# Attention pairs interleaved on TensorE, group factors taken ahead of the output product, and two moved steps in the second block, in a two-block transformer kernel

## What is computed

```python
h = rms_norm(x, g_mix_norm[l])
z = h @ w_in[l]                      # latents, rope key, u and v of a gating unit, pool input
a  = mla_mixer(...)                  # 4 heads of causal softmax attention, width 512
gm = sgu_mixer(uv, ...)              # u * (W @ rms_norm(v) + b), width 256
po = pool_mixer(pin, ...)            # windowed means, then a 64x64 product per group, width 256
mix = concatenate([rms_norm(a, g1), rms_norm(gm, g2), rms_norm(po, g3)])
x = x + mix @ w_out[l]
h = rms_norm(x, g_ffn_norm[l])
x = x + (silu(h @ w_gate[l]) * (h @ w_up[l])) @ w_down[l]
```

## Time and profile before

| | us |
|---|---|
| median of 3 runs | 3214.23 (3213.72 to 3214.51) |
| the profiled execution | 3211.73 |
| its span in the profile | 3209.9 |
| PE busy | 3129.9 (98%) |
| POOL busy | 1905.3 (59%) |
| DVE busy | 1486.2 (46%) |
| ACT busy | 736.1 (23%) |

### The profile page before, as it was taken

One profiled execution on the slowest core, in us unless ns is written; L12 is line 12 of the kernel. 1 busy time (PEld: TensorE's weight loads), 2 busy tenths in 40 slices (PEclk: granted clock), 3 DMA queues, 4 the chain that ended last, 5 costly groups with the idle time before them and its releaser, 6 DMA issues.

```text
span 3209.9 us, 41968 instructions
## 1 busy us (share of the span) xinstructions
PE 3129.9 (98%) x15408; PEld 2512.8 (78%) x15408; DVE 1486.2 (46%) x2570; ACT 736.1 (23%) x1521; POOL 1905.3 (59%) x885
## 2 busy tenths in 40 slices
PE   8899999989999999999999999999999999999998
PEld 7588888868888878877588888887787658888887
DVE  4654530365543033886554555212288654554521
ACT  4410000432010032434711101012243470111000
POOL 4267777427787777001078777787700118877785
PEclk9999999999999999999999999999999999999999
DMA  3122333113223222112022232232211202333232
GB/s 122 47 94 93 97 98 98 54 46 100 93 97 98 96 83 96 48 40 73 14 90 94 101 98 97 93 99 86 92 47 34 79 10 97 99 101 97 93 98 85
DMA packets 71716, 262.99 MB, mean 82 GB/s; under 512 B 8208, under 2 KB 8208, under 8 KB 71440
## 3 DMA queue, kind: packets, MB, share of 16 engines
q1 hardware_dynamic: 71280, 258.86, 24.8%
q10 hardware_dynamic: 288, 2.11, 0.2%
HBM read 258.85 MB, written 2.10 MB: 81 GB/s over the span
## 4 chain that ended last, share of the span: by engine, by line
PE 64%; POOL 16%; issue 13%; DVE 6%; ACT 1%; POOLq 0%; DVEq 0%; ACTq 0%
PE bank L633 63%; POOL w_hi L1377 9%; POOL w_lo L1383 6%; PE bank L1240 1%; DVE arena L1914 1%; DVE rope L1911 0%; DVE arena L2443 0%; ACT arena L1851 0%; DVE arena L1911 0%; DVE arena L2271 0%; DVE arena L2459 0%; DVE w_lo L2297 0%; DVE rope L1914 0%; ACT arena L1837 0%; POOL act_hi L1377 0%
## 5 line engine op out<-in xcount | busy, mean ns | idle before, releaser
L1377 POOL TENSOR_TENSOR w_hi<-ring,one 128x1024 fp32r<-128x1024 f32 x430 | 822.0, 1912 | 1239.2 <-PE bank L633 1184.5
L1383 POOL TENSOR_TENSOR w_lo<-ring,w_hi 128x1024 fp32r<-128x1024 f32 x422 | 1038.5, 2461 | 33.1
L633 PE MATMUL bank<-h_hi,w_hi 128*128 128x512 f32 x2256 | 895.8, 397 | 4.6 <-DVE h_lo L1938 2.5
L633 PE MATMUL bank<-h_hi,w_lo 128*128 128x512 f32 x2256 | 881.3, 391 | 0.0
L633 PE MATMUL bank<-h_lo,w_hi 128*128 128x512 f32 x2256 | 880.6, 390 | 0.0
L633 PE MATMUL bank<-act_hi,w_hi 128*128 128x512 f32 (+1 forms) x1392 | 517.5, 400 | 10.7 <-issue 8.9
L633 PEld LDWEIGHTS bank<-h_hi,w_hi 128*128 128x128 f32 x2256 | 424.2, 188 | 99.3 <-issue 5.5
L633 PEld LDWEIGHTS bank<-h_hi,w_lo 128*128 128x128 f32 x2256 | 424.1, 188 | 91.2
L633 PEld LDWEIGHTS bank<-h_lo,w_hi 128*128 128x128 f32 x2256 | 424.5, 188 | 84.7 <-issue 1.0
L633 PE MATMUL bank<-act_hi,w_lo 128*128 (+1 forms) x1120 | 442.0, 395 | 0.0
L633 PE MATMUL bank<-act_lo,w_hi 128*128 (+1 forms) x1104 | 416.3, 391 | 1.4 <-DVE act_lo L2478 1.4
(11 more groups left out here) (243 smaller groups left out, 3002.6 us busy)
## 6 DMA issues: line engine op xcount, KB each, us to landing
ring<-wstream SPq DMA_DIRECT2D x480, 512.0 KB, 3.5
par<-params SPq DMA_DIRECT2D x4, 656.5 KB, 6.1
x<-xT SPq DMA_DIRECT2D x4, 512.0 KB, 7.7
outT<-h SPq DMA_DIRECT2D x4, 512.0 KB, 2.7
cst<-const ACTq DMA_DIRECT2D x1, 1412.0 KB, 9.4
par<-params ACTq DMA_DIRECT2D x1, 652.5 KB, 5.5
arena<-pos SPq DMA_DIRECT2D x1, 256.0 KB, 2.6
cst<-const SPq DMA_DIRECT2D x1, 24.5 KB, 2.5
```

What stands on the lines that cost most here:

```text
L633: return pe.matmul(out, lhsT, rhs, start=start, stop=stop)
L1377: return po.tensor_tensor(out, a, one.broadcast_to([P, n]), ALU.mult)
L1383: po.tensor_tensor(pair_[1], raw, pair_[0].bitcast(F32), ALU.subtract).then_inc(done.sem, 1)
```

## The change

The diff, cut, with eight columns of indentation taken off:

```diff
-mix_hi, mix_lo = u_hi, u_lo
+mix_hi = [act_hi[:, 20 + c, :] for c in range(2)] + u_hi[2:]
+mix_lo = [act_lo[:, 13, :]] + u_lo[1:]
...
+def z_bank(g):
+    return bank[6] if g == 18 else bank[g % 3]
+def pool_bank(b):
+    return bank[(7, 1)[b]]
...
-        def dense(g, s):
-            pe.wait_ge(*w1_split(l, s + 1 if g else 0))
-            z_wait(g)
-            for k in range(ND):
+        def dense(g, s, blocks=range(ND)):
+            if 0 in blocks:
+                pe.wait_ge(*w1_split(l, s + 1 if g else 0))
+                z_wait(g)
+            for k in blocks:
                 if g == 0 and k == ND // 2:
                     pe.wait_ge(*w1_split(l, 1))
                 if g == 0:
                     pe.wait_ge(*u_ready(l, k + 1))
-                last = block_product(bank[g % 3][:, :], weights1(s), k, u_hi[k], u_lo[k], k == 0, k == ND - 1)
-            last.then_inc(z_mm.sem, 1)
+                last = block_product(z_bank(g)[:, :], weights1(s), k, u_hi[k], u_lo[k], k == 0, k == ND - 1)
+            if ND - 1 in blocks:
+                last.then_inc(z_mm.sem, 1)
...
+            if st == 0:
+                pe.wait_ge(*at_c(l, w + 1))
+            for e in range(2):
+                c = 8 * w + 2 * st + e
...
-        score_pair(0)
-        score_pair(1)
-        dense(18, 9)
-        pe.wait_ge(*z_out(l, 19))
-        turn_pair(0)
-        pe.wait_ge(*at_m(l, 8))
-        pe.wait_ge(*sg_v(l, NT))
-        pe.wait_ge(*sg_w(l, 4))
-        for b in range(2):
+        def gated(b):
...
+        score_pair(0)
+        score_pair(1)
+        pe.wait_ge(*z_out(l, 18))
+        turn_pair(0, 0)
+        pe.wait_ge(*at_m(l, 7))
+        pe.wait_ge(*sg_v(l, NT))
+        pe.wait_ge(*sg_w(l, 4))
+        gated(0)
+        turn_pair(0, 1)
+        gated(1)
+        turn_pair(0, 2)
+        turn_pair(0, 3)
         pv_pair(0)
-        turn_pair(1)
+        turn_pair(1, 0)
+        pe.wait_ge(*at_m(l, 8))
+        dense(18, 9, (0, 1))
+        dense(18, 9, (2, 3))
+        turn_pair(1, 1)
+        dense(18, 9, (4, 5))
+        turn_pair(1, 2)
+        dense(18, 9, (6, 7))
+        turn_pair(1, 3)
         for b in range(2):
             pe.wait_ge(*pl_m(l, b + 1))
-            product(bank[6 + b][:, :], par[:, PAR1["w_pool"]][:, b * P:b * P + P],
+            if b:
+                pe.wait_ge(*at_o(l, 16))
+            product(pool_bank(b)[:, :], par[:, PAR1["w_pool"]][:, b * P:b * P + P],
                     m1["win_m"][:, b, :]).then_inc(pl_mm.sem, 1)
         pv_pair(1)
...
         pe.wait_ge(*pl_o(l, 2))
+        pe.wait_ge(*z_out(l, 19))
         mix_sum(1)
         mix_spread(0)
         mix_spread(1)
+        mix_sum(2)
...
-        pe.wait_ge(*mx_n(l, 4))
-        pe.wait_ge(*wo_r(l, 6))
+        pe.wait_ge(*wo_r(l, 4))
         for j in range(2):
             pe.wait_ge(*w1_split(l, 10 + j + 1))
-            out_part(j, 0, rest_bank(j)).then_inc(wo_a.sem, 1)
-        mix_sum(2)
+            out_part(j, 1, heads_bank(j)).then_inc(wo_a.sem, 1)
+        mix_spread(2)
         pe.wait_ge(*wo_r(l, ND))
-        out_part(0, 1, heads_bank(0)).then_inc(wo_mm.sem, 1)
-        mix_spread(2)
-        out_part(1, 1, heads_bank(1)).then_inc(wo_mm.sem, 1)
+        for j in range(2):
+            out_part(j, 0, rest_bank(j)).then_inc(wo_mm.sem, 1)
...
+        for t in range(NT):
+            exp_pair(0, t)
+        exp_pair(1, 0)
+        exp_pair(1, 1)
+        copy_pair(0, 0)
+        exp_pair(1, 2)
+        copy_pair(0, 1)
+        exp_pair(1, 3)
+        copy_pair(0, 2)
+        copy_pair(0, 3)
+        for c in range(2):
+            out_square(c)
+            out_high(c)
+        for st in range(NT):
+            copy_pair(1, st)
         copy_z(18, m1["u"][:, 1, :])
-        copy_pair(0)
-        pair_out(0)
-        copy_pair(1)
         for b in range(2):
...
-            sc.activation(mixsq[:, 6 + b, :], bank[6 + b][:, :], ACT.Square, scale=col).then_inc(pl_q.sem, 1)
-            sc.activation(mix[:, 6 + b, :], bank[6 + b][:, :], ACT.Copy, scale=col).then_inc(pl_o.sem, 1)
+            sc.activation(mixsq[:, 6 + b, :], pool_bank(b)[:, :], ACT.Square, scale=col).then_inc(pl_q.sem, 1)
+            sc.activation(mix[:, 6 + b, :], pool_bank(b)[:, :], ACT.Copy, scale=col).then_inc(pl_o.sem, 1)
...
+        for c in (2, 3):
+            out_square(c)
...
+        for c in (2, 3):
+            out_high(c)
...
-        pair_out(1)
...
+        def prefix_exp(u, v):
+            m = (1 << v) >> 1
+            c9, lf = 9 * u + v, LIN[u][3]
+            if v == 1:
+                sc.wait_ge(*(hf_l(l, u + 1) if u < 4 else gl_f(l, u - 3)))
+            else:
+                sc.wait_ge(*ln_p(l, 8 * u + v - 1))
+            if c9 > 2:
+                sc.wait_ge(*ln_q(l, c9 - 2))
+            sc.activation(compact(m2["Eq"][c9 % 2], m), halves(lf, m, 1), ACT.Exp).then_inc(ln_e.sem, 1)
         for key in YKEYS[17:BEFORE]:
             copy_out(key)
+            if key == ("gog", 1):
+                prefix_exp(0, 1)
         def out_copy(hd):
             if hd >= 2:
...
-                if v == 1:
-                    sc.wait_ge(*(hf_l(l, u + 1) if u < 4 else gl_f(l, u - 3)))
-                else:
-                    sc.wait_ge(*ln_p(l, c8))
-                if c9 > 2:
-                    sc.wait_ge(*ln_q(l, c9 - 2))
-                sc.activation(compact(m2["Eq"][c9 % 2], m), halves(lf, m, 1), ACT.Exp).then_inc(ln_e.sem, 1)
...
+                    prefix_exp(u, v)
                 if u > 0 and v in (1, 2):
...
-        mask_pair(0)
-        mask_pair(1)
-        scale_pair(0)
-        ve.wait_ge(*pl_r(l, 2))
-        pool_means(0)
-        scale_pair(1)
-        low_part_of(0)
-        low_part_of(1)
-        pool_means(1)
-        assert steps[0] == pw.per, steps[0]
-        for b in range(2):
+        def gate_values(b):
...
+        mask_pair(0, range(NT))
+        mask_pair(1, (0, 1))
+        scale_pair(0)
+        mask_pair(1, (2, 3))
+        scale_pair(1)
+        ve.wait_ge(*pl_r(l, 2))
+        pool_means(0)
+        gate_values(0)
+        low_part_of(0)
+        pool_means(1)
+        ve.wait_ge(*z_mm(l, 19))
+        low_part_of(1)
+        assert steps[0] == pw.per, steps[0]
+        gate_values(1)
...
-        for n in range(2, ND):
-            low_part_of(n)
+        low_part_of(2)
+        low_part_of(3)
         ve.wait_ge(*mx_sd(l, 3))
         inverse(mx_rc, four(mx_rstd, 2), four(mx_std, 2))
+        for n in range(4, ND):
+            low_part_of(n)
...
-            if j < 2:
-                ve.wait_ge(*wo_a(l, j + 1))
-                add(x[:, j, :], x[:, j, :], rest_bank(j)[:, :]).then_inc(wo_b.sem, 1)
-                ve.wait_ge(*wo_mm(l, j + 1))
-                ve.wait_ge(*mx_c(l, 1))
-                second = heads()
-            else:
-                ve.wait_ge(*wo_a(l, j + 1))
-                add(x[:, j, :], x[:, j, :], heads()).then_inc(wo_b.sem, 1)
-                ve.wait_ge(*wo_mm(l, j + 1))
-                second = rest_bank(j)[:, :]
+            ve.wait_ge(*mx_c(l, 1))
+            ve.wait_ge(*wo_a(l, j + 1))
+            add(x[:, j, :], x[:, j, :], heads()).then_inc(wo_b.sem, 1)
+            ve.wait_ge(*wo_mm(l, j + 1))
+            second = rest_bank(j)[:, :]
...
         for j in range(ND):
+            if j % 2 == 0:
+                ve.wait_ge(*y_mm(l, 4 + j // 2))
             ve.wait_ge(*hh_t(l, j + 1))
             ve.tensor_tensor(h_lo[:, j, :], low_part[:, j, :], h_hi[:, j, :].bitcast(F32), ALU.subtract)\
```

More of the change, by code:

```diff
@@ L1556, in copy_z @@
                     if square is not None:
-                        sc.activation(square, bank[g % 3][rows, :], ACT.Square).then_inc(done.sem, 1)
-                    sc.activation(dst, bank[g % 3][:, :], ACT.Copy).then_inc(z_out.sem, 1)
+                        sc.activation(square, z_bank(g)[rows, :], ACT.Square).then_inc(done.sem, 1)
+                    sc.activation(dst, z_bank(g)[:, :], ACT.Copy).then_inc(z_out.sem, 1)
                 for c in range(2):
@@ L1591, in mixer1 @@
                 copy_z(17, m1["u"][:, 0, :])
-                def exp_pair(w):
-                    for t in range(NT):
-                        sc.wait_ge(*at_m(l, NT * w + t + 1))
-                        for e in range(2):
-                            c = 8 * w + 4 * e + t
-                            p_ = nprob[w][e][:, PS0[t]:PS0[t] + (t + 1) * P]
-                            last = sc.activation(p_, p_, ACT.Exp, bias=small[:, c:c + 1], scale=-1.0,
-                                                 accum_out=small[:, 16 + c:17 + c])
-                        last.then_inc(at_e.sem, 1)
@@ L1620, in mixer1, with exp_pair @@
-                exp_pair(0)
-                exp_pair(1)
+                def exp_pair(w, t):
+                    sc.wait_ge(*at_m(l, NT * w + t + 1))
+                    for e in range(2):
+                        c = 8 * w + 4 * e + t
+                        p_ = nprob[w][e][:, PS0[t]:PS0[t] + (t + 1) * P]
```

(24 more changed lines are left out.)

35 lines of the change are left out of this document (9 added, 26 removed).

## The result

The changed kernel takes 3190.27 us (median of 3 runs, 3186.69 to 3193.49), the kernel before 3214.23 us: a ratio of 0.9924, interval 0.9910 to 0.9937. The forecast was 3182.7 us with a range of 3171 to 3196. The sign and the range hold, the gain is 7.5 us short. With the runs of two later groups (12 runs of the changed kernel in all, 3182.7 to 3193.5) the median is 3185.9 us, so about 28 of the 31.5 us are there.

The account below looks back on a forecast made before the run. PE was taken to bound the kernel, through gaps and half clock. Attention stages 21.0, second-block entries 8.9 and linear attention 1.6 sum to 31.5 us: 3180.2 us profiled, 3182.7 us as median, range 3171 to 3196.

Parts of the forecast that it names:

- What bounds the kernel: PE, busy 3129.9 of 3209.9 us; with its work unchanged, only gaps and half-clock time can change.
- First part of the stage: Attention stage up to the end of pair 1's values product: 31.0 to 25.5 us, 5.5 us less.
- The 1.2 us wait on the last transposes of pair 0: ACT's copies stand behind pair 1's last exponential and release these transposes late, so PE waits 1.2 us.
- The tightest place: At `mix_sum(0)`, block 5's multiplication on DVE was to end with POOL's split, leaving PE 1 us to spare.
- The low halves of blocks 2 and 3: Before the output product: their chain ends 8.9 us after the values product, PE arrives at 9.0; no wait, bound 0.5.
- Second part: From pair 1's values product to output block 2: 30.9 to 22.8 us, 8.1 us less, before half clock.
- The wait at block 2: PE waits for tile 12's split ahead of output block 2: 2.0 us instead of 0.91.
- the 2.5 us for half clock: Allowance per layer for half clock around the sums: 1.7 under dense work plus 0.8, bounds 0 and 6.2 us.
- the first rival: The sums lower the clock as before, 6.2 us a layer lost instead of 2.5: 3190.1 us; chance 0.14.
- the second clock rival: Pair 0's transposes lower the clock for 3.4 us under the values product, losing 1.7 us a layer: 3186.1 us; chance 0.08.
- Entry of the second block: Pairing `h_lo` removes PE's 3.26 us wait and half clock behind it, less 0.9: gains 5.0 and 4.0 us.
- Start of the linear attention: DVE's first product comes 10 us early, PE's wait shrinks and moves: 0.8 us a layer, 1.6 us in all.

Follow-up runs that it names:

- the first repeat: The changed kernel run again unaltered, for its spread: 3185.84 us, ratio 0.9914 of the kernel before.
- filling: Against the changed kernel, twelve full output-product matmuls moved between the sums, six behind the first and six ahead of the third: 3182.72 us, again 3178.59 us.
- without the exponentials: The changed kernel with twelve matmuls moved between the sums, but ScalarE's early exponentials undone: 3179.47 us, again 3177.63 us.
- the entry alone: The kernel before with only VectorE's eight h_lo low halves waiting in pairs at the second block's entry: 3208.88 us, ratio 0.9982.
- the early exponentials alone: The kernel before with only ScalarE's first two linear-attention exponentials moved ahead of the last output copies: 3218.10 us, ratio 1.0017.

## Why the prediction was right, and where it was short

- **What bounds the kernel**: right. In the stretches read above all of the time that came or went is idle time of PE or half clock of PE. Over the whole execution PE's idle time fell from 71.6 us to 51.0, 50.4 and 50.6 in the three profiles, which is the sum of the parts (13.6 in the stages, 6.5 at the entries, 0.9 at the linear attention); by how much more or less the executions gained goes with their clock.
- **First part of the stage**, 31.0 to 25.5 us forecast: 24.3 us at a clock of 1.00. The 1.2 us wait on the last transposes of pair 0 was 0.26. The tightest place, `mix_sum(0)`, held: DVE's multiplication of block 5 (132.56) came just as POOL's high half ended and took 0.69 us, not the length of a split. The low halves of blocks 2 and 3 brought no wait either.
- **Second part**, 30.9 to 22.8 us and some half clock: 29.2 us. The instructions and the wait came out as summed: take off what half clock added (3.2 us in the third sum, 0.8 in the spreads, 12 output matmuls at 0.20, together 6.4) and 22.8 us are left. The wait at block 2 was 1.81 for 2.0.
- **The step that failed** is the 2.5 us for half clock in this part. It was 6.4 us, at and just over the upper bound of 6.2. The prediction had the right row in hand: half clock behind `mix_sum(2)` with no gap ahead of it, "such sums lower the clock as idling does". But it priced the new stretch as if a lost clock were met by dense matmuls only for 3.4 us, when its own list puts 3.5 us of sums, 2 us of spreads and 3.5 us of sums in a row, 9 us. And it priced half clock by full matmuls alone; one-column matmuls take twice as long too. This is the mechanism of the first rival ("the sums take the clock as before", 3190.1 us, 0.14). That the first three runs lie at its time is luck: the step costs 7.8 us in two layers, the first part of the stage and the entries give 4.3 more than forecast, and what the first profile lacks besides is mostly half clock in the second layer's scores, which no sum had. That the twelve runs lie only 3 us from the forecast is in part such a balance too.
- **Transposes**: the second clock rival fell. Behind the new stretch of transposes and gating products the values products ran at a clock of 1.00 in both layers of the first repeat, and in the window 112.47:136.74 above. The Trainium skill ("TensorE: Matmul & The Clock Gate", "Part 4: PE-mode transpose") says that they don't count as activity; in this kernel the clock did not fall behind them. Where it was at half already, from the scores, it came back 2.4 to 5.7 us into the new stretch (seven layers), against 2.5 us into `dense(18, 9)` in the one such layer of the old order; whether the transposes hold it down longer isn't shown.
- **Entry of the second block**, 5.0 and 4.0 us: 5.8 and 5.0 us in the profile of the change, 5.8 and 4.9 alone. The pairs cost PE nothing instead of 0.9 us a layer: the split beside a pair took 2.40 + 0.08 + 2.73 = 5.2 us, 0.85 more than by itself, which is under the 1.07 us that the prediction found to spare. It had put the pair's full 1.22 us on top of the split, 0.15 more than the slack; four times that is 0.6, where it has 0.9. The rows show how: the engines alternate. POOL's high half goes behind DVE's first low half, DVE's second (0.6 us of work) behind POOL's high half, so the pair spans 2.99 us. The Trainium skill ("SBUF — State Buffer", "SBUF: two separate sides") calls the shared ports an exclusive lock held for an instruction at a time; these rows agree.
- **Start of the linear attention**, 0.8 us a layer: 0.45 us less idle time, nothing in the runs. The first profile gained 1.9 us at each of the two places, since it has no half clock there, the first repeat 0.3. The wait went on to the second and third level, as forecast; the half clock behind it came twice as long when the edit stood alone.
- **The sum, as measured**: the stage 8.4 us in each layer where the scores ran at full clock, 16.8; the entries 10.8; idle time at the linear attention 0.9. That is 28.5 us, and the median of twelve runs lies 28.3 below that of before. So close an agreement is chance, given how far single medians stray from their places above. In the first profile 10 us less are seen (18.2 at the end): 4.2 were lost up to the end of the second layer's scores, and its stage, entered at half clock, gained 4.1 instead of 8.4.

**What stays open.** By the traces, filling saves 6.2 us of stage in a layer, 12.4 in both; the pooled medians show 4 us (8 without the exponentials), those of the last group 6.8. 2.7 of it is the wait at block 2, which is shorter in every profile. It is the same with the entry alone (10.7 us at its places, 5.1 in the median) and the early exponentials alone (1.0 us lost at its places, 4.1 in the median). Half clock in the two stages together was 27 to 36 us in the three profiles of the changed kernel and 3 to 13 in the five of the kernels with all twelve matmuls moved; but outside the stages it was 47 us on average in the former and 57 in the latter (30 to 79). Whether that is the chance of a few profiles, or whether a clock kept up in one place falls more easily in another, these runs don't tell. Why the scores fall to half clock in 8 of 28 layers, with the same instructions ahead of them, wasn't found either; three of the four profiles of the version with two sixes have it in the first layer, some 35 us ahead of the first moved matmul.

## What to carry to other kernels

Price a reordering at both clocks: list what PE runs in a row without a full matmul in it, count one-column sums and their broadcasts as idle time for the clock, and give their own durations twice over, not those of the dense work behind them alone. When a wait is closed by moving such sums together, part of the gain is paid back; spread them through the dense work instead, which costs no instruction and here made the stage 6.2 us shorter than the reordering alone. And a small operation put beside another engine's work costs only what exceeds the slack of that period.

## What the runs showed of the hardware

- Thirty-two matmuls of one column took 3.63 us at the full clock and 6.83 us at half, so they follow the clock although each moves one column; and while nothing but such sums and broadcasts of 128 columns runs, the clock goes down with PE busy all the time (136.74:141.30: busy 4.56 of 4.56 us, then granted 0.50 from 141.30 on).
- The same kernel differs from one execution to the next by where the clock falls. In the changed kernel's three profiles the half clock adds up to 91.1, 71.2 and 74.9 us; over all runs here 0.001 more of the mean granted clock went with 2.7 us less time. The kernel before ran from 3204.9 to 3221.9 us (41 runs), far more than the 0.8 us between its first three runs. A difference of under 5 us between two kernels needs more than one group of runs, and the place in the trace is the better witness.
